# A two-layer mixer and a gated state-space block on one core: both recurrences without the identity products between their level products

## The reference, cut to what matters

```python
def step(state, inp):
    qc, kc, vc, lf = inp
    a = jnp.cumsum(lf, axis=2)
    a_last = a[:, :, -1:, :]
    s_new = jnp.exp(a_last)[:, :, 0, :, None] * state + jnp.einsum(
        "bhsk,bhsv->bhkv", kc * jnp.exp(a_last - a), vc)
    inter = jnp.einsum("bhtk,bhkv->bhtv", qc * jnp.exp(a), state)
    diff = a[:, :, :, None, :] - a[:, :, None, :, :]
    dec = jnp.exp(jnp.where(causal, diff, -jnp.inf))
    scores = jnp.einsum("bhtk,bhsk,bhtsk->bhts", qc, kc, dec)
    intra = jnp.einsum("bhts,bhsv->bhtv", scores, vc)
    return s_new, inter + intra
```

## Time and profile before

| | us |
|---|---|
| median of 3 runs | 4190.99 |
| lowest and highest run | 4185.57, 4193.89 |
| the profiled execution, its own time | 4189.99 |
| span of the profiled execution | 4188.1 |
| PE busy over the span | 3779.4 (90%) |
| DVE busy over the span | 2659.9 (64%) |
| mean granted TensorE clock | 0.951 |

### The profile page before, as it was taken

One profiled execution on the slowest core, in us unless ns is written; L12 is line 12 of the kernel. 1 busy time (PEld: TensorE's weight loads), 2 busy tenths in 40 slices (PEclk: granted clock), 3 DMA queues, 4 the chain that ended last, 5 costly groups with the idle time before them and its releaser, 6 DMA issues. The chain is left out here.

```text
span 4188.1 us, 57647 instructions
## 1 busy us (share of the span) xinstructions
PE 3779.4 (90%) x21712; PEld 2922.3 (70%) x21712; DVE 2659.9 (64%) x4025; ACT 1961.5 (47%) x3606; POOL 958.9 (23%) x1088
## 2 busy tenths in 40 slices
PE   6989888989998887987889999989988989999998
PEld 5775677877775665766646666667756778888886
DVE  3756466976766467966555555546976666566655
ACT  4544355444554275344434444445644554444444
POOL 0016102630006102610045555600093000101000
PEclk7999999989999998998999999999999999999999
DMA  5100112664210111023100000022002551111244
GB/s 187 41 16 1 45 43 75 233 220 171 81 40 1 43 38 63 2 96 113 30 5 6 5 10 5 21 82 78 11 13 72 213 171 51 41 61 41 106 151 146
DMA packets 211398, 295.98 MB, mean 71 GB/s; under 512 B 74218, under 2 KB 140010, under 8 KB 211124
## 3 DMA queue, kind: packets, MB, share of 16 engines
q1 hardware_dynamic: 210564, 292.09, 21.0%
q0 software_dynamic: 416, 0.05, 0.0%
q10 hardware_dynamic: 144, 0.15, 0.0%
HBM read 261.65 MB, written 30.51 MB: 70 GB/s over the span
## 5 line engine op out<-in xcount | busy, mean ns | idle before, releaser
L533 DVE TENSOR_TENSOR x_low<-buf_a,x_high 128x640 fp32r<-128x640 f32 (+5 forms) x360 | 357.6, 993 | 388.6 <-ACT x_high L581 385.8
L581 ACT CAST x_high<-buf_a 128x640 fp32r<-128x640 f32 (+5 forms) x360 | 311.2, 865 | 501.6 <-PE ps L641 429.5
L639 PE MATMUL ps<-x_high,w_high 128*128 128x512 f32 (+1 forms) x1184 | 451.5, 381 | 94.4 <-DVE w_low L537 87.9
L640 PE MATMUL ps<-x_low,w_high 128*128 128x512 f32 (+1 forms) x1184 | 439.9, 372 | 0.0
L641 PE MATMUL ps<-x_high,w_low 128*128 128x512 f32 (+1 forms) x1184 | 438.7, 371 | 0.0
L3237 PE MATMUL ps<-w_high,x_high 128*128 128x512 f32 x896 | 362.9, 405 | 63.6 <-DVE w_low L3067 59.5
L3239 PE MATMUL ps<-w_high,x_low 128*128 128x512 f32 x896 | 357.3, 399 | 0.0
L3238 PE MATMUL ps<-w_low,x_high 128*128 128x512 f32 x896 | 356.8, 398 | 0.0
L639 PEld LDWEIGHTS ps<-x_high,w_high 128*128 128x128 f32 x1184 | 228.9, 193 | 164.3 <-DVE x_low L533 109.8
L3067 DVE TENSOR_TENSOR w_low<-w,w_high 128x1024 fp32r<-128x1024 f32 x170 | 208.0, 1224 | 176.7 <-ACT w_high L3185 176.5
L3807 DVE TENSOR_REDUCE mx<-ps 128x1 fp32r<-128x1280 f32 x128 | 190.7, 1491 | 199.9 <-PE ps L3682 199.4
(11 more groups left out here) (446 smaller groups left out, 8888.6 us busy)
## 6 DMA issues: line engine op xcount, KB each, us to landing
w<-in_w_out SPq DMA_DIRECT2D x26, 2048.0 KB, 8.4
w<-in_w_mod SPq DMA_DIRECT2D x24, 2048.0 KB, 9.2
w<-in_w_down SPq DMA_DIRECT2D x15, 2048.0 KB, 7.8
w<-in_w_in SPq DMA_DIRECT2D x26, 1024.0 KB, 5.6
w<-in_w_up SPq DMA_DIRECT2D x22, 1024.0 KB, 7.7
w<-in_w_in SPq DMA_DIRECT2D x6, 2048.0 KB, 8.9
x<-in_x SPq DMA_DIRECT2D x16, 512.0 KB, 9.0
scratch_h<-x SPq DMA_DIRECT2D x8, 512.0 KB, 6.2
```

The lines of the kernel that those rows point to most:

```text
L533: dve.tensor_tensor(xl[i % NX][:, 0:s["tn"]], x_of(s), xh[i % NX][:, 0:s["tn"]].bitcast(F32), ALU.subtract).then_inc(x_low, 1)
L581: act.copy(xh[i % NX][:, 0:s["tn"]], x_of(s)).then_inc(x_high, 1)
L639: pe.matmul(g["out"], lhs[0][:, :], rhs[0][:, :], start=(s["kk"] == 0), stop=False)
L640: pe.matmul(g["out"], lhs[0][:, :], rhs[1][:, :], start=False, stop=False)
```

## The change

`keep_busy` and its two call lines are taken out. Nothing else is changed, and every other instruction keeps its place on its engine.

```diff
-            def keep_busy(u, g):
-                if g == 1:
-                    pe.wait_ge(D2[1].o_out, n_out[u])
-                pe.matmul(ps[:, 6, P:HALF], k.ident[:, :], D2[0].masks[:, 0:3, :], start=True, stop=True)
-
             for u in range(NU):
                 if not want[u]:
                     for r in D2:
@@
                             turn_keys(r, u)
                         if g == 1:
                             states(r, u)
-                        if g and not (mods and g >= 2):
-                            keep_busy(u, g)
                     if mods and g >= 2:
                         pe.wait_ge(D2[g - 2].state_out, u + 1)
                         mods.products(pe, mods.first + 2 * u + g - 2)
```

## The result

| | before | changed |
|---|---|---|
| median of 4 runs, us | 4189.66 | 4212.81 |
| lowest and highest, us | 4185.57, 4193.89 | 4209.05, 4218.34 |
| the profiled execution, us | 4189.99 | 4209.05 |
| its span, us | 4188.1 | 4207.2 |
| mean granted clock | 0.951 | 0.939 |

What follows compares the result with a forecast made beforehand. It took a unit to be bound by a ring of DVE's work in g=1 to 3 and PE's chain in g=0. Half-clock cost +31.5 less gains 5.7 gave +26 us on 4189.99, about 4216, median 4217; range 4192 to 4240.

Steps and rivals of the forecast that it cites:

- the forecast case: Second recurrence: the clock falls in g=2 or g=3, is half through g=0, returns in g=1; 4208 to 4226 us, chance 0.38.
- the second rival: Second recurrence: the clock falls but returns early, about half of each g=0 slow; 4201 us (4194 to 4208), chance 0.22.
- The middle units lie beside DVE: Middle units of both recurrences: DVE's copies and scalings cover the identity products (5.0 us a second-recurrence unit); removal gains nothing.
- The three uncovered places: Gains: second recurrence's last unit 4.1 us, first's last unit 1.6, first's first unit 0 (bounds -1.5, +1.5); -5.7 us total.
- The first recurrence keeps its clock: First recurrence: no fall expected, since the products of `mods` remain behind g=2 and g=3 and fill 2.2 us each.
- Where the clock falls: Second recurrence, g=2 or g=3: only level products remain, leaving PE idle about 5.3 us out of 9.7 in each unit.
- the list 1.97, 1.48, 0.95 and 0.95 us: Second recurrence, g=2 and g=3: PE's expected waits after 1.09 us of work in each step paced by DVE's copies.
- The price of a passage: Second recurrence, g=0 of both directions at half clock: 10.5 us in place of 6.0, so +4.5 us each time.
- How many passages: Second recurrence, units 3 to 9: 7 passages through g=0 at half clock, 7 x 4.5 = +31.5 us.
- The sum: Whole kernel: +31.5 - 5.7 = +26 us on the profiled execution's 4189.99, about 4216; median 4217.
- The case in which the clock never comes back: Second recurrence: g=1 slow too, +5.9 us for each of 7 passages, last unit +3; +43 us, 4234, chance 0.20.
- The rival made from it, that the clock stays full: Second recurrence: clock holds at 1.00 over 1680 to 1800 us; 4185 us, or 4183 with the first unit's gain; chance 0.16.

## Why the prediction was right

The forecast was 4217 us for the median, in a range of 4192 to 4240, from a fall of the clock in the second recurrence. The median is 4212.8. The case that happened is the forecast case; two of its seven passages went as in the second rival.

- **The middle units lie beside DVE.** Right in the main. At an unchanged clock, removing the products left a unit nearly as it was: 19.25 us against 19.4 in the first recurrence, and 18.85 against 19.15 in the second where only those of g=3 stayed. I had counted nothing, which leaves out 1.1 us over the eight full units of the first recurrence. Of the 0.3 us in the second, 0.22 are shorter DVE instructions (below); in the first, DVE's scaling of keys (line 1072) fell from 647 to 517 ns, and why was not tested.
- **The three uncovered places.** First recurrence, last unit: 1.6 us predicted, 1.7 measured (18.7 to 17.0). First unit: 0, within 1.5, predicted; from the memset to the first outputs 29.1 us against 29.9, a gain of 0.7. Second recurrence, last unit: 4.1 us predicted at full clock, 4.0 measured in the kernel that spares it alone.
- **The first recurrence keeps its clock.** Right: 1.00 over 740 to 896 us in every kernel without its identity products whose trace can be read.
- **Where the clock falls.** In g=3, as the sum had it, but by waits that I had put in the wrong place. The wrong step is the list 1.97, 1.48, 0.95 and 0.95 us, which sets each level product beside DVE's copies of its own group. PE starts a group as soon as the copies of the group before are done, so the waits are 0.45 us before the second direction's g=2, 1.33 and 2.05 us before the two of g=3, and then 0.47 us before the outputs at half clock (1.40 at full clock, as the kernel with g=2 alone shows). The sum of about 5.3 us was right (5.2 at full clock); the order was not. It did not matter for the time and it cost me the two wrong expectations on g=2 and g=3.
- **The price of a passage.** For a g=0 at half clock I had 10.5 us in place of 6.0; it is 10.46. L1206 holds PE 1.90 us in the first direction and 1.73 in the second (I took 1.7 for both), the turned keys 0.49 and 0.62. That the sum of 10.5 came out so exactly is in part errors that cancel.
- **How many passages.** 7 of 4.5 us, 31.5 in all, were predicted. Six intervals give +5.2, +5.1, +2.4, +1.9, +4.6 and +4.7 us, and the seventh, +1.1, is 5.1 for the passage less 4.0 for the last unit. That is 28.9 us in all: the mechanism was right and this term was 2.6 us too large. Two passages were cheap because the full clock was back within g=0, as in the second rival. These are the second direction's outputs in the third and in the fourth passage, where half clock gives 1.80 us:

```profile
1727.47 1.62 PE L1206 MATMUL ps<-v,sc 128*128 128x64 f32 x8
...
1749.00 1.12 PE L1206 MATMUL ps<-v,sc 128*128 128x64 f32 x8
```

- **The sum.** It was made for the profiled execution, +26 us, and that one shows +19.1, the lowest of its four; between the medians it is 23.2. The 7 us are 2.6 of the passages, 2.1 of the first recurrence (3.7 gained where 1.6 was counted) and 2.5 outside both recurrences, where nothing was changed; the second recurrence's other parts take back 0.4. That the median came nearer than this execution is luck.
- **Small slips that change nothing.** DVE's waits for PE over the 130 us of the earlier trace rows add up to 8.7 us, not "some 10". The case in which the clock never comes back adds up to +42.4, not +43. And the range starts at 4192, so it takes in all of the early-back case (4194 to 4208), not its upper part.
- **The page's rule.** The Trainium skill, "TensorE: Matmul & The Clock Gate", warns in "Why this matters for your kernels" of a long idle gap between bursts. The rival made from it, that the clock stays full, was refuted: the clock fell behind waits of 2.05 us at most, and in one kernel behind waits of 1.39 us at most. The same page's section "A second HAM failure mode: psum-queue depth-cycling" tells of another kernel, in which frequent short idling between groups of matmuls made the clock swing between its levels. The trace agrees with that: such a swing is in every unit, for instance 0.50 over 1674 to 1687 us and 0.91 in the 4.5 us behind it.

## What to carry to other kernels

A product whose result nobody reads can be worth its time where PE has slack. Before taking it out, look at what PE would do there instead, and not at whether it is on the path: many short waits close together can cost the clock, and the price is then paid later, in the stretch where PE is the bound. And such products may be needed only where the waits collect: with an engine that runs a step ahead of the one it waits for, that is a step later than it seems. Here 14 of 68 did the whole work, in the group before the chain that PE sets, and the other 54 cost about 7 us.

## What was not expected

The loss repeats itself to the tenth of a microsecond. The second recurrence began up to 7.1 us apart in the spans of three kernels (the changed one, that with products in the first recurrence alone, and that with the wait alone). Yet all three show the same intervals: 24.3 or 24.4, 24.2 or 24.3, 21.5, 21.0, 23.8, 23.8, 19.4 or 19.5 us. The fall of the clock and the program's pace seem to lock to each other. Three starts are few, and I did not try what sets this, for instance by a delay ahead of the stage.

With the products of g=1 gone, DVE's multiplications by queries and keys are shorter, at the same shape and count. In six units of the kernel with products in g=3 alone, and then in those of the kernel before (count | busy, mean ns):

```profile
L1081 DVE TENSOR_TENSOR x<-x,qk 128x256 f32<-128x256 f32 x85 | 40.9, 515 | 0.0
```
```profile
L1081 DVE TENSOR_TENSOR x<-x,qk 128x256 f32<-128x256 f32 x85 | 41.8, 526 | 0.0
```

That is 0.15 us of the 0.3 us that a unit gains; line 1072 gives 0.07 more. The kernel that keeps g=2 and g=3 shows the same (40.8 us, and units of 18.85 us), so it is the products of g=1 that matter. Without them the level products end earlier, so POOL, which waits for them, subtracts at another time beside DVE. That the two share something is argued from this and was not tested.
